# The closing counts of a top-k selection moved into the stage that attends

## The reference

```
score = einsum('bth,bths->bts', wi * IDX_HEADS ** -0.5, relu(dots))
score = where(visible, score, -inf)
vals, idx = lax.top_k(score, n_sel)                     # n_sel = 256
logits = einsum('bthd,btkhd->bthk', q, ks) * A_HEAD_DIM ** -0.5
p = softmax(where(valid, logits, -inf)); o = einsum('bthk,btkhd->bthd', p, vs)
```

## Time and profile before

| | us |
|---|---|
| runs | 4721.47, 4724.14, 4727.0 (median 4724.14) |
| the profiled execution | 4714.88 |
| its span | 4713.2 |
| PE busy in the span | 3909.2 (83%) |
| DVE busy | 2078.6 (44%) |
| ACT busy | 1671.5 (35%) |
| POOL busy | 768.9 (16%) |

### The profile page before, as it was taken

One profiled execution on the slowest core, in us unless ns is written; L12 is line 12 of the kernel. 1 busy time (PEld: TensorE's weight loads), 2 busy tenths in 40 slices (PEclk: granted clock), 3 DMA queues, 4 the chain that ended last, 5 costly groups with the idle time before them and its releaser, 6 DMA issues. The chain is left out here.

```text
span 4713.2 us, 55090 instructions
## 1 busy us (share of the span) xinstructions
PE 3909.2 (83%) x20365; PEld 3271.3 (69%) x20365; DVE 2078.6 (44%) x3267; ACT 1671.5 (35%) x2860; POOL 768.9 (16%) x518
## 2 busy tenths in 40 slices
PE   8989993565888887199367888669999999979999
PEld 7889993222777776188364444369999999956676
DVE  3255503785899997697413343241211212221111
ACT  5522111554999997155102222221111111121110
POOL 0032222220444432220300000022112122000000
PEclk9999996555999998599659999779999999989999
DMA  3212124001011110210521111101111111052221
GB/s 114 84 54 76 72 76 103 29 4 57 28 45 38 38 43 24 63 28 16 160 101 37 43 53 43 57 33 56 55 37 55 47 45 55 28 188 78 70 85 51
DMA packets 176881, 279.18 MB, mean 59 GB/s; under 512 B 30253, under 2 KB 136661, under 8 KB 166205
## 3 DMA queue, kind: packets, MB, share of 16 engines
q1 hardware_dynamic: 165532, 262.36, 17.3%
q0 software_dynamic: 3328, 8.40, 0.6%
q10 hardware_dynamic: 7856, 6.36, 0.5%
HBM read 188.89 MB, written 88.86 MB: 59 GB/s over the span
## 5 line engine op out<-in xcount | busy, mean ns | idle before, releaser
L1840 ACT ACTIVATE sl_junk<-sc_score,sl_nfb 128x640 bf16<-128x640 f32 (+12 forms) x416 | 577.1, 1390 | 0.0
L2945 DVE TENSOR_SCALAR fu_acc<-fu_raw,fu_extra 128x2048 f32<-128x2048 f32 x22 | 28.3, 1287 | 741.8 <-ACT fu_up L2912 741.8
L156 PE MATMUL fu_p_g<-fu_hn_hi,fu_w_hi 128*128 128x412 f32 (+1 forms) x880 | 306.9, 349 | 20.1 <-POOL fu_w_lo L2899 20.1
L156 PE MATMUL fp_p_o<-fp_hn_hi,fp_w_hi 128*128 128x412 f32 (+1 forms) x840 | 295.0, 351 | 18.4 <-POOL fp_w_lo L482 18.4
L156 PE MATMUL fu_p_g<-fu_hn_hi,fu_w_lo 128*128 128x412 f32 (+1 forms) x880 | 309.0, 351 | 0.0
L156 PE MATMUL fu_p_u<-fu_hn_hi,fu_w_lo 128*128 128x412 f32 (+1 forms) x880 | 308.5, 351 | 0.0
L156 PE MATMUL fu_p_g<-all_hn_lo,fu_w_hi 128*128 128x412 f32 (+1 forms) x880 | 307.8, 350 | 0.0
L156 PE MATMUL fu_p_u<-all_hn_lo,fu_w_hi 128*128 128x412 f32 (+1 forms) x880 | 306.8, 349 | 0.0
L156 PE MATMUL fu_p_u<-fu_hn_hi,fu_w_hi 128*128 128x412 f32 (+1 forms) x880 | 306.0, 348 | 0.0
L156 PE MATMUL fp_p_o<-fp_hn_hi,fp_w_lo 128*128 128x412 f32 (+1 forms) x840 | 294.0, 350 | 0.0
L156 PE MATMUL fp_p_o<-h_hn_lo,fp_w_hi 128*128 128x412 f32 (+1 forms) x840 | 292.9, 349 | 0.0
(11 more groups left out here) (528 smaller groups left out, 8818.6 us busy)
## 6 DMA issues: line engine op xcount, KB each, us to landing
scratch_act<-fu_acc SPq DMA_DIRECT2D x22, 1088.0 KB, 4.9
fu_w<-in_w_gu SPq DMA_DIRECT2D x22, 1024.0 KB, 6.9
fd_a<-scratch_act SPq DMA_DIRECT2D x17, 960.0 KB, 5.8
scratch_conv<-fp_acc SPq DMA_DIRECT2D x14, 1028.0 KB
fp_w<-in_w_fm SPq DMA_DIRECT2D x21, 512.0 KB, 3.7
scratch_tm<-np_out SPq DMA_DIRECT2D x17, 524.0 KB, 2.7
np_x<-in_x SPq DMA_DIRECT2D x17, 512.0 KB, 3.9
fd_x<-scratch_x SPq DMA_DIRECT2D x17, 512.0 KB, 6.9
```

Source lines behind the costliest of these rows:

```text
L156: last = pe.matmul(out, a, b, start=k == 0, stop=k == n - 1)
L1840: act.activation(self.junk[0:p, j % 2, 0:w], src, ACT.Sign, bias=self.nfb[0:p, n:n + 1].bitcast(F32), accum_out=self.cnt[0:p, n:n + 1]).th ...
L2945: dve.tensor_scalar(a, raw[:, 2:2 + SEQ], taps(i.t, 2), None, ALU.mult)
```

## The change

- `stage_threshold` is gone as a stage. Its instructions are now `threshold_ops`, which DVE runs in the block of `stage_attend`, ahead of its first mask. Its `junk` is now the same memory as the logits, masks and `eq` of the attention (a tile `work`, of which `L`, `mb` and `eq` are views).
- DVE no longer subtracts in the splitting of the keys. POOL does (8 subtractions of 64x1024), and ACT takes over the rounding of the top (4 copies of 64x2048) from POOL. `part` has two buffers: ACT may be one half head ahead of POOL.
- `sel.junk` and `sel.low`, outputs of the counts in the scan that nobody reads, are allocated in the scan's scope, to make room; the selection's other tiles now live until the attention's end, and so does its scope `sl` with its semaphores.

```diff
-def stage_threshold(nc, sel, thr, room):
-    with Scope(nc, "se") as s:
...
+def threshold_ops(dve, link, sel, junk, lo, carry, thr, room):
+    key, cand, tmp, fb, cnt = sel.key, sel.cand, sel.tmp, sel.fb, sel.cnt
+    def count(op, value):
+        for n in range(NSEL):
+            src = block_of(sel.score, n)
+            p = src.shape[0]
+            ins = dve.tensor_scalar(block_of(junk, n), src, value[0:p, n:n + 1], None, op, ALU.add,
+                                    accum_out=cnt[0:p, n:n + 1])
+        link(ins)
...
+    link(dve.tensor_scalar(room[:], cnt[:], -1.0, float(TOPK), ALU.mult, ALU.add))
...
-        part = s.sb("part", [P, SEQ // 2], F32R)
+        part = s.sb("part", [P, 2, SEQ // 2], F32R)
-        L = s.sb("L", [P, 3, SEQ])
-        mb = s.sb("mb", [P, 2, SEQ], BF16)
-        eq = s.sb("eq", [P, SEQ], BF16)
+        work = s.sb("work", [P, 9 * CHUNK * 2])
+        L = work[:, 0:3 * SEQ].rearrange("p (r n) -> p r n", n=SEQ)
+        mb = work[:, 3 * SEQ:4 * SEQ].bitcast(BF16).rearrange("p (r n) -> p r n", n=SEQ)
+        eq = work[:, 4 * SEQ:9 * CHUNK * 2].bitcast(BF16)
+        junk = work[:].bitcast(BF16)
...
                 pool.wait_ge(c_k, 32 * AH)
-                for h in range(AH):
-                    pool.tensor_tensor(k[top, h], k32[top, h], one[top].broadcast_to([AD, SEQ]),
-                                       ALU.mult).then_inc(c_khi, 1)
+                pool.wait_ge(c_qs, 2)
+                for n, (h, cols) in enumerate(k_parts):
+                    pool.wait_ge(c_part, n + 1)
+                    pool.tensor_tensor(k[bottom, h, cols], k32[bottom, h, cols], part[bottom, n % 2].bitcast(F32),
+                                       ALU.subtract).then_inc(c_low, 1)
+                pool.wait_ge(c_low, len(k_parts))
...
                 for n, (h, cols) in enumerate(k_parts):
-                    wait(act, c_low, n)
-                    act.activation(part[bottom], k32[bottom, h, cols], ACT.Copy).then_inc(c_part, 1)
+                    wait(act, c_low, n - 1)
+                    act.activation(part[bottom, n % 2], k32[bottom, h, cols], ACT.Copy).then_inc(c_part, 1)
+                    if n % 2:
+                        act.activation(k[top, h], k32[top, h], ACT.Copy).then_inc(c_khi, 1)
...
-                for n, (h, cols) in enumerate(k_parts):
-                    dve.wait_ge(c_part, n + 1)
-                    dve.tensor_tensor(k[bottom, h, cols], k32[bottom, h, cols], part[bottom].bitcast(F32),
-                                      ALU.subtract).then_inc(c_low, 1)
+                threshold_ops(dve, Link(dve, c_thr), sel, junk, lo, carry, thr, room)
                 mask(0, range(5))
...
                     stage_scan(nc, A, gates, masks, sel)
-                    stage_threshold(nc, sel, thr, room)
-                stage_attend(nc, A, masks, score, thr, room)
+                    stage_attend(nc, A, masks, sel, score, thr, room)
```

More of the change, by code:

```diff
@@ L750, in stage_scan @@
         yT = s.sb("yT", [P, 4, P])
+        sel.buffers(s)
         b_a, b_b, b_c, b_d, b_m, b_1, b_2, b_3 = (s.ps(n, [P, 4 * P]) for n in
@@ L1788, in __init__, with buffers @@
         self.bits = s.sb("bits", [P, 32], I32)
+        self.c_here, self.made = s.sem("here"), 0
+        self.c_small, self.c_cand, self.c_act = s.sems("small", 2), s.sems("cand", 2), s.sem("act")
+    def buffers(self, s):
         self.junk = s.sb("junk", [P, 2, SEQ], BF16)
         self.low = s.sb("low", [P, P * (SEL[HERE - 1] + 1)], BF16)
-        self.c_here, self.made = s.sem("here"), 0
-        self.c_small, self.c_cand, self.c_act = s.sems("small", 2), s.sems("cand", 2), s.sem("act")
     def loads(self, A):
@@ new lines, in threshold_ops @@
+def threshold_ops(dve, link, sel, junk, lo, carry, thr, room):
[7 more added lines that the diff above has]
+        link(ins)
+    link(dve.tensor_single_scalar(lo[:], key[:], 0xFFFF, ALU.bitwise_and))
+    link(dve.tensor_scalar(lo[:], lo[:], 1.0, None, ALU.add))
+    link(dve.tensor_single_scalar(carry[:], lo[:], 16, ALU.logical_shift_right))
+    link(dve.tensor_single_scalar(lo[:], lo[:], 0xFFFF, ALU.bitwise_and))
+    link(dve.tensor_single_scalar(cand[:], key[:], 16, ALU.logical_shift_right))
+    link(dve.tensor_tensor(cand[:], cand[:], carry[:], ALU.add))
+    link(dve.tensor_single_scalar(cand[:], cand[:], 16, ALU.logical_shift_left))
+    link(dve.tensor_tensor(cand[:], cand[:], lo[:], ALU.bitwise_or))
+    sel.as_float(dve, link)
+    count(ALU.is_ge, fb[:].bitcast(F32))
+    sel.enough(dve, link, 1)
+    link(dve.tensor_tensor(carry[:], key[:], cand[:], ALU.bitwise_xor))
+    link(dve.tensor_tensor(carry[:], carry[:], tmp[:], ALU.bitwise_and))
+    link(dve.tensor_tensor(cand[:], key[:], carry[:], ALU.bitwise_xor))
+    sel.as_float(dve, link)
+    link(dve.memset(thr[:, NSEL - 1:NSEL], 0.0))
+    dve.tensor_copy(thr[:, 0:NSEL - 1].bitcast(I32), fb[:, 0:NSEL - 1])
+    link(dve.tensor_copy(thr[0:NB, NSEL - 1:NSEL].bitcast(I32), fb[0:NB, NSEL - 1:NSEL]))
+    count(ALU.is_gt, thr[:])
+    link(dve.tensor_scalar(room[:], cnt[:], -1.0, float(TOPK), ALU.mult, ALU.add))
@@ L1918, in mask_ops, with stage_attend @@
             link(dve.tensor_scalar(dst, dst, 1.0, MASKED, ALU.subtract, ALU.mult))
-def stage_attend(nc, A, masks, score, thr, room):
+def stage_attend(nc, A, masks, sel, score, thr, room):
     with Scope(nc, "at") as s:
@@ L1930, in stage_attend @@
         k32, k = s.sb_twin("k", [P, AH, SEQ])
-        part = s.sb("part", [P, SEQ // 2], F32R)
+        part = s.sb("part", [P, 2, SEQ // 2], F32R)
         one = s.sb("one", [P, 1])
         v = s.sb("v", [P, PT, AH * AD])
-        L = s.sb("L", [P, 3, SEQ])
-        mb = s.sb("mb", [P, 2, SEQ], BF16)
-        eq = s.sb("eq", [P, SEQ], BF16)
+        work = s.sb("work", [P, 9 * CHUNK * 2])
[3 more added lines that the diff above has]
+        junk = work[:].bitcast(BF16)
+        lo, carry = s.sb("lo", [P, NSEL], I32), s.sb("carry", [P, NSEL], I32)
+        c_thr = s.sem("threshold")
         cum = s.sb("cum", [P, SEQ])
```

## The result

| | median of the runs, us | lowest to highest | ratio to before |
|---|---|---|---|
| before | 4725.57 | 4721.47 to 4731.12 (4 runs) | |
| after | 4671.38 | 4669.44 to 4678.01 (4 runs) | 0.9887 [0.987, 0.9904] |

The changed kernel is faster by 54.2 us, 1.1%. The forecast was 4670 us (range 4657 to 4688) with a saving of 54.2 us.

What follows compares the result with a forecast made beforehand. PE idled 107.1 us until the keys were split. Starting it 55.2 us earlier, less 0.7 and 0.3, saves 54.2 us; off the median 4724.14 that makes 4669.9, say 4670 us, range 4657 to 4688.

Steps and rivals of the forecast that it cites:

- The start of the block: Attention block's loads start at 1882.36 in place of 1929.64, 47.3 us earlier; keys land 26.4 us into the block.
- The counts beside POOL: DVE's second round of threshold counts runs beside POOL's subtractions; neither slows the other, costed at nothing.
- Rival 1: DVE's counts and POOL's subtractions slow each other in the splitting: gain 40.6 - 1.0 us, time 4684.5; chance 0.07.
- The splitting: Eight POOL subtractions of the keys at 2.40 us plus seven gaps of 0.07 take 19.7 us, ending at 1929.6.
- PE's start: PE starts the attention's first logits at 1929.6 in place of 1984.8, 55.2 us earlier.
- Which path is last: Before the first logits, POOL's path (47.2 us) ends later than DVE's counts (46.2 us), leaving DVE 1.4 us of margin.
- What comes back: Losses: 0.7 us for block 1's mask conversion waiting for POOL, 0.3 for scope `sl`'s exit behind the attention.
- The clock: PE's clock in the early attention takes the same course as before, 0.50 then 0.93: neither gain nor loss.
- Rival 4: PE's clock stays at 0.50 through the attention: +198 - 54 = 144 us, time 4868; chance 0.03.
- Rival 3: The block's loads wait until the counts are done; only the splitting gains, 7.9 us, time 4716; chance 0.02.
- The time: Whole kernel: saving of 54.2 us off the timed median 4724.14 makes 4669.9, say 4670 us.
- Rival 2: Five small DVE operations between the counts wait for POOL's subtractions, 11.5 us on DVE's path: time 4680.4; chance 0.04.

Runs made afterwards that it cites:

- experiment 1: Kernel before with only the new splitting of the keys (POOL subtracts, ACT rounds the top), closing counts still their own stage: 4713.78 us, ratio 0.998.
- experiment 2: Changed kernel with the splitting of before (POOL multiplies, DVE subtracts, now behind its counts): 4685.11 us, ratio 0.9925.
- Experiment 3: Changed kernel with the keys' DMAs issued by ACT, not by SP behind the queries: 4679.2 us, ratio 0.9906.
- experiment 4: Changed kernel with the keys' DMAs issued by ACT and POOL waiting until DVE has written the thresholds: 4669.32 us, ratio 0.9891.
- experiment 8: Experiment 4 with the sample group's second count at the loop's end, masks of blocks 0 and 1 before the threshold, block 1's loads behind the keys: 4667.86 us.

## Why the prediction was right

- **The start of the block**, 47.3 us earlier: the two starts coincide. The keys came 26.7 us into the block, forecast 26.4.
- **The counts beside POOL**, costed at nothing: right to 2 ns. Rival 1 is out; experiments 1 and 2 show the other side of it, POOL's durations with and without the counts.
- **The splitting**, 19.7 us for eight subtractions: measured 18.53. Each is recorded with 2.35 to 2.37 us, near the 2.40 of the row, but they start 2.31 us apart: the gap of 0.07 between two did not occur. The estimate from the Trainium skill ("GPSIMD Engine Reference", side-by-side cycle accounting), 2.25 for one, makes 18.5 with that gap; it comes out because its two errors, the short duration and the gap, cancel.
- **PE's start**: 1984.82 - 1882.36 = 102.5 us into the block before, 1929.55 - 1883.05 = 46.5 after. 56.0 us sooner, forecast 55.2: the keys and the first subtraction 0.4 later, the subtractions 1.2 shorter.
- **Which path is last**: the forecast said POOL's, with 1.4 us of margin for DVE. It was DVE's, narrowly. The operation on `mx_room` took 0.43 us for 0.17, and block 0's conversion, L2101, took 0.94 where it had been 0.23: POOL's last subtraction and then its queries shut them out. The first logits came 1.18 us after PE's start, before 0.83. I had costed this mask at its old duration and the shut-out only in block 1's, at 0.7; block 1's conversion took 0.47, 0.24 more than alone.
- **What comes back**, 0.7 + 0.3: measured 56.0 - 54.6 = 1.4 us. The two conversions are most of what I can place: PE's matmul of block 1 came 4.40 us after its start, before 3.81, 0.6 us. From DVE's last operation (2214.21 + 0.42, before 2268.36 + 0.42) to the next stage's load it is 3.2 us, before 2.9: that is the 0.3 of the scope's exit. The other 0.5 lie in the loop, and I don't resolve them. The queries were ready 2.4 us after PE's start, as forecast, and nothing waited for them.
- **The clock**: 0.50 up to PE's start, then 0.64, 0.70 and 0.98 over the next 15, 15 and 30 us, and 1.00. The kernel before had 0.50, 0.72 and 1.00 over the same stretches: nearly the same course, and both have a mean of 0.96 up to the next stage. Rival 4 is out. Rival 3 is out with the first row of the timeline.
- **The time**: 54.6 us in the block, 54.2 in the medians, 54.2 forecast. That the last two agree to a tenth is luck; the medians of a kernel differ by some us from one series to the next. What was wrong is the forecast of a span near 4659: it took the rest of the profiled execution of before for granted, which was 9.8 us shorter behind the block. Taking the saving off the median, not off that execution, kept this out of the time. Every run of the changed kernel lies in the range of 4657 to 4688.

Rival 2 did not happen, but it was close. The small operations ended 25.0 us into the block, and POOL's first subtraction came at 27.9. Experiment 3 used up that margin of 2.9 us, and the first logits came 6.1 us later.

## What to carry to other kernels

A stage in which one engine works alone can be laid beside another's loads and preparation at almost no cost if the work is handed to engines that neither queue behind it nor share with it; moving it without handing the preparation over left 17 us. Where two paths then end together, look at the small operations at their seams, and measure how far the other engine's start is from them: a load that lands sooner can make the next step later. Work that an idle stretch hides is not free inside a busy loop, where 21 us of it cost 24 to 36 us of the block in one profile each and 15 to 27 in the medians.

## What was not expected of the hardware

- Operations with one input were shut out by a two-input subtraction on POOL for its whole length: 128x15 int32 `tensor_scalar` 2.27 us for 0.17, a 128x14 copy 2.15. MEMSET (0.06 and 0.11) and the accumulating counts were not.
- Loading the keys on a second queue beside the queries made the queries late: POOL waited 22.2 us for them, where it was 6.6 with both on one queue (experiments 3, 4 and 8 against the changed kernel, run twice).
- One kernel's runs spread over 20 us (4704.65 to 4724.66 in experiment 1), and between profiles differences go with the granted clock: a stretch with the same 1790 matmuls took 499.3 us at 0.98 and 505.2 at 0.96.
